# The first feed-forward group summed ahead of the norm, in the mixer projection's stage

## The reference, cut to what matters

```python
mixed = gates[:, :, 0] * y_ssm + gates[:, :, 1] * y_rwkv + gates[:, :, 2] * y_hgrn
x = x + mixed @ w_out[l]
h_gate, h_up = jnp.split(rmsnorm(x, norm2_w[l]) @ ffn_w_in[l], 2, axis=-1)
x = x + (jax.nn.silu(h_gate) * h_up) @ ffn_w_down[l]

def rmsnorm(x, w, eps=NORM_EPS):
    xf = x.astype(jnp.float32)
    y = xf * lax.rsqrt(jnp.mean(xf * xf, axis=-1, keepdims=True) + eps)
    return (y * w.astype(jnp.float32)).astype(x.dtype)
```

## Time and profile before

| | |
|---|---|
| median of 3 runs | 2075.53 us (2075.15 to 2080.94) |
| the profiled execution | 2076.96 us, span 2075.0 us |
| mean granted TensorE clock | 0.971 of full speed |
| TensorE busy | 1925.8 us, 93% of the span |
| VectorE, ScalarE busy | 1019.0 us (49%), 602.2 us (29%) |
| HBM traffic | 88 GB/s over the span |

### The profile page before, as it was taken

How to read it: one execution, slowest core, us unless ns; L and a number is a source line. 1 busy time by engine, 2 the same in 40 slices (tenths; PEclk the granted TensorE clock), 3 DMA queues, 4 the chain that set the end, 5 groups by cost and what they waited for, 6 DMA issues and landing times. The chain is left out here.

```text
span 2075.0 us, 40175 instructions
## 1 busy us (share of the span) xinstructions
PE 1925.8 (93%) x16700; PEld 1418.4 (68%) x16700; DVE 1019.0 (49%) x2050; ACT 602.2 (29%) x1287; POOL 75.3 (4%) x51
## 2 busy tenths in 40 slices
PE   6989999999999999998988799978898999989998
PEld 2566666666666666544666687767774998878887
DVE  3456666667676767312135568675445452311101
ACT  2234343434444443302023233233333220000000
POOL 0001010101010101000000000010000000000000
PEclk9999999999999999999999899989999999999999
DMA  9021213111111012022211433230002222534343
GB/s 379 24 83 45 100 52 104 41 63 41 33 42 32 32 42 73 1 92 101 102 66 41 156 122 122 83 121 33 33 33 112 82 82 81 183 122 149 139 178 142
DMA packets 52240, 184.73 MB, mean 89 GB/s; under 512 B 5856, under 2 KB 9312, under 8 KB 51552
## 3 DMA queue, kind: packets, MB, share of 16 engines
q1 hardware_dynamic: 52064, 182.23, 24.0%
HBM read 180.11 MB, written 2.10 MB: 88 GB/s over the span
## 5 line engine op out<-in xcount | busy, mean ns | idle before, releaser
L845 PE MATMUL banks<-u,w_ring 128*128 128x512 f32 x768 | 361.8, 603 | 2.0 <-DVE u L681 2.0
L386 PE MATMUL banks<-u,w_ring 128*128 128x256 f32 x1056 | 250.1, 389 | 8.4 <-PEq L195 8.4
L386 PEld LDWEIGHTS banks<-u,w_ring 128*128 128x128 f32 x1056 | 199.1, 195 | 41.9 <-issue 17.0
L845 PEld LDWEIGHTS banks<-u,w_ring 128*128 128x128 f32 x768 | 139.2, 192 | 124.5 <-issue 117.2
L410 PE MATMUL banks<-u,w_ring 128*128 128x256 f32 x704 | 155.0, 384 | 4.8 <-PEq L195 4.8
L410 PEld LDWEIGHTS banks<-u,w_ring 128*128 128x128 f32 x704 | 135.7, 193 | 24.0 <-issue 5.0
L3351 PE MATMUL banks<-gated,w_ring 128*128 128x512 f32 (+1 forms) x288 | 96.8, 498 | 1.8 <-PEq L195 1.8
L873 DVE SCALAR_TENSOR_TENSOR acc<-raw,hc,acc 128x512 f32<-128x512 f32 x128 | 96.2, 752 | 4.5
L3351 PEld LDWEIGHTS banks<-gated,w_ring 128*128 128x128 f32 x288 | 54.6, 190 | 44.1 <-issue 40.8
L3351 PE MATMUL banks<-ffn,w_ring 128*128 128x256 f32 x352 | 77.9, 385 | 3.0 <-PEq L195 3.0
L3201 DVE SCALAR_TENSOR_TENSOR ffn_tanh<-ffn_tanh,banks 128x256 f32<-128x256 f32 x22 | 9.2, 417 | 138.0 <-ACT ffn_tanh L3193 138.0
(11 more groups left out here) (500 smaller groups left out, 3202.0 us busy)
## 6 DMA issues: line engine op xcount, KB each, us to landing
w_ring<-in_w SPq DMA_DIRECT2D x289, 512.0 KB, 5.6
gated<-in_ada SPq DMA_DIRECT2D x32, 512.0 KB, 4.5
h<-in_h SPq DMA_DIRECT2D x2, 2048.0 KB, 9.6
const_base<-in_const SPq DMA_DIRECT2D x1, 1216.0 KB, 5.4
hold<-h SPq DMA_DIRECT2D x1, 1024.0 KB, 5.2
const_part<-in_const SPq DMA_DIRECT2D x1, 1024.0 KB, 4.9
h<-hold SPq DMA_DIRECT2D x1, 1024.0 KB, 9.6
out<-u SPq DMA_DIRECT2D x8, 128.0 KB, 1.9
```

The lines of the kernel that those rows point to most:

```text
L386: mm = self.nc.tensor.matmul(place, self.st.chunk(g % 2, slot)[:, P * k:P * k + P], self.src(k), start=(k == 0), stop=(k == KT - 1))
L845: mm = nc.tensor.matmul(self.places[m % len(self.places)][:, :], (st.slot(m) if g is None else st.chunk(g % 2, m))[:, P * k:P * k + P], u[ ...
```

## The change

A new tile `root` (128 x 256) is set aside. In `mixer_out` ScalarE also makes h x norm2_w for each of the 8 feature tiles and puts it into columns 0 to 255 of u. TensorE multiplies the first feed-forward group's four chunks with it, into banks 0 to 3: one tile, then the column sums; one tile, then the transposes; then two tiles more. ScalarE copies the spread root from bank 7 to `root`, and the eight products for u read it from there. `swiglu` has ten groups left. Its VectorE first multiplies the four finished banks with `root` and, with ScalarE's tanh, forms the first two tiles of the output. Banks are numbered anew so that the four are free when needed, and the ring's groups are split 7 and 10 where they were 6 and 11.

```diff
+        root = sb("root", [P, SEQ])
...
-def swiglu(nc, st, bank, src, out, th):
+def swiglu(nc, st, bank, src, out, th, root):
-    count = FF // 2
+    count = FF // 2 - 1
...
         def tensor(pe):
             def visit(g, h, r):
-                if not isinstance(g, int) or g >= 2:
-                    pe.wait_ge(s["done"], g * 2 - 2)
+                if not isinstance(g, int) or g >= 1:
+                    pe.wait_ge(s["done"], g * 2)
                 for m in range(4):
                     st.wait(pe, h, r, m)
-                    mm = accumulate(nc, bank[4 * h + m][:, 0:SEQ], [st.chunk(h, m)[:, P * k:P * k + P] for k in range(KT)],
+                    mm = accumulate(nc, bank[4 - 4 * h + m][:, 0:SEQ], [st.chunk(h, m)[:, P * k:P * k + P] for k in range(KT)],
...
         def scalar(act):
+            for m in range(2):
+                act.wait_ge(s["rooted"], 2 * m + 2)
+                nc.scalar.activation(out[:, m, :], th[:, 0, m, :], ACT.Tanh, scale=0.5).then_inc(s["rough_tanh"], 1)
...
         def vector(dve):
+            for m in range(2):
+                for up in range(2):
+                    nc.vector.tensor_tensor(th[:, up, m, :], bank[2 * up + m][:, 0:SEQ], root, ALU.mult).then_inc(s["rooted"], 1)
+            for m in range(2):
+                dve.wait_ge(s["rooted"], 2 * m + 2)
+                dve.wait_ge(s["rough_tanh"], m + 1)
+                nc.vector.scalar_tensor_tensor(out[:, m, :], out[:, m, :], 1.0, th[:, 0, m, :], ALU.add, ALU.mult).then_inc(s["doubled"], 1)
+                dve.wait_ge(s["doubled"], m + 1)
+                nc.vector.scalar_tensor_tensor(out[:, m, :], out[:, m, :], 0.5, th[:, 1, m, :], ALU.mult, ALU.mult).then_inc(s["done"], 1)
...
     units = [(b, m) for b in range(4) for m in range(KT)]
-    through = [0, 4, 8, 16, 24, 28, 32]
+    place = lambda q: (q + 4) % banks
+    through = [0, 4, 8, 16, 24, 28, 32, 33]
...
-        st.in_stage(6, 4, s["used"], block, through, {3: reload})
+        st.in_stage(7, 4, s["used"], block, through, {3: reload})
...
-            tail.sums(pe)
+
+            def rough(c):
+
+                st.wait(pe, 6 % 2, 6 // 2, c)
+                pe.wait_ge(s["evacuated"], len(units) - banks + c + 1)
+                for k in range(KT):
+                    if c == 0:
+                        pe.wait_ge(s["primed"], k + 1)
+                    mm = nc.tensor.matmul(bank[c][:, 0:SEQ], st.chunk(6 % 2, c)[:, P * k:P * k + P], u[:, k, 0:SEQ],
+                                          start=(k == 0), stop=(k == KT - 1))
+                return mm
+
+            rough(0)
+            pe.wait_ge(s["added"], KT - 1)
+            column_sums(nc, C, bank[7], tail.acc, tail.tiles).then_inc(s["sums"], 1)
+            rough(1)
+            pe.wait_ge(s["root"], 1)
+            spread(nc, C, bank[7], tail.rs, tail.tiles).then_inc(s["spread"], 1)
+            rough(2)
+            rough(3).then_inc(s["used"], 1)
 
         @block.scalar
         def _(act):
             link = Chain(act, s["act_own"])
             for k in range(KT):
+                act.wait_ge(s["evacuated"], 3 * KT + k + 1)
+                link(nc.scalar.activation(u[:, k, 0:SEQ], tail.tile(k), ACT.Copy, scale=g_cols[:, k:k + 1]), s["primed"])
                 tail.square(act, link, k)
+            act.wait_ge(s["spread"], 1)
+            link(nc.scalar.activation(root, bank[7][:, 0:SEQ], ACT.Copy), s["copied"])
...
             tail.mean(dve, link)
-            tail.scale(dve, link, u, g_cols)
-
-    st.passed(6, 4)
+            dve.wait_ge(s["copied"], 1)
+            tail.scale(dve, link, u, g_cols, root)
+
+    st.passed(7, 4)
```

More of the change, by code:

```diff
@@ L3143, in build @@
         with ExitStack() as es:
-            mixer_out(nc, st, bank, C, (ys, yr, yh), early, gates, h, hold, late, tail_work(SEQ, es), u, cc("norm2_w"))
+            mixer_out(nc, st, bank, C, (ys, yr, yh), early, gates, h, hold, late, tail_work(SEQ, es), u, cc("norm2_w"), root[:, :])
             nc.sync.sem_clear(late)
@@ L3150, in build @@
             ffn_tanh = sb("ffn_tanh", [P, 2, 2, SEQ], es)
-            swiglu(nc, st, bank, latent, ffn, ffn_tanh)
+            swiglu(nc, st, bank, latent, ffn, ffn_tanh, root[:, :])
             def add(m, ps, link, done):
@@ L3168, in build @@
         st.drain()
-def swiglu(nc, st, bank, src, out, th):
-    count = FF // 2
+def swiglu(nc, st, bank, src, out, th, root):
+    count = FF // 2 - 1
     st.begin(4)
-    with stage(nc, "used tanh doubled done") as (s, block):
+    with stage(nc, "rooted rough_tanh used tanh doubled done") as (s, block):
         def tensor(pe):
             def visit(g, h, r):
-                if not isinstance(g, int) or g >= 2:
-                    pe.wait_ge(s["done"], g * 2 - 2)
+                if not isinstance(g, int) or g >= 1:
+                    pe.wait_ge(s["done"], g * 2)
                 for m in range(4):
                     st.wait(pe, h, r, m)
-                    mm = accumulate(nc, bank[4 * h + m][:, 0:SEQ], [st.chunk(h, m)[:, P * k:P * k + P] for k in range(KT)],
+                    mm = accumulate(nc, bank[4 - 4 * h + m][:, 0:SEQ], [st.chunk(h, m)[:, P * k:P * k + P] for k in range(KT)],
                                     [src(k) for k in range(KT)])
@@ L3187, in scalar @@
         def scalar(act):
+            for m in range(2):
+                act.wait_ge(s["rooted"], 2 * m + 2)
+                nc.scalar.activation(out[:, m, :], th[:, 0, m, :], ACT.Tanh, scale=0.5).then_inc(s["rough_tanh"], 1)
             def visit(g, h, r):
                 act.wait_ge(s["used"], g + 1)
-                if not isinstance(g, int) or g >= 2:
-                    act.wait_ge(s["done"], g * 2 - 2)
+                act.wait_ge(s["done"], max(g * 2, 2) if isinstance(g, int) else g * 2)
                 for m in range(2):
-                    nc.scalar.activation(th[:, h, m, :], bank[4 * h + m][:, 0:SEQ], ACT.Tanh, scale=0.5).then_inc(s["tanh"], 1)
+                    nc.scalar.activation(th[:, 1 - h, m, :], bank[4 - 4 * h + m][:, 0:SEQ], ACT.Tanh, scale=0.5).then_inc(s["tanh"], 1)
             walk(act, count, visit)
         def vector(dve):
+            for m in range(2):
[7 more added lines that the diff above has]
+                nc.vector.scalar_tensor_tensor(out[:, m, :], out[:, m, :], 0.5, th[:, 1, m, :], ALU.mult, ALU.mult).then_inc(s["done"], 1)
             def visit(g, h, r):
@@ L3200, in visit @@
                     dve.wait_ge(s["tanh"], g * 2 + 2)
-                    nc.vector.scalar_tensor_tensor(th[:, h, m, :], th[:, h, m, :], 1.0, bank[4 * h + m][:, 0:SEQ],
+                    nc.vector.scalar_tensor_tensor(th[:, 1 - h, m, :], th[:, 1 - h, m, :], 1.0, bank[4 - 4 * h + m][:, 0:SEQ],
                                                    ALU.add, ALU.mult).then_inc(s["doubled"], 1)
-                    dve.wait_ge(s["doubled"], g * 2 + (m + 1))
-                    nc.vector.scalar_tensor_tensor(out[:, bass.ds(g * 2 + m, 1), :].rearrange("p a t -> p (a t)"), th[:, h, m, :], 0.5,
-                                                   bank[4 * h + 2 + m][:, 0:SEQ], ALU.mult, ALU.mult).then_inc(s["done"], 1)
+                    dve.wait_ge(s["doubled"], g * 2 + (m + 3))
+                    nc.vector.scalar_tensor_tensor(out[:, bass.ds(g * 2 + (2 + m), 1), :].rearrange("p a t -> p (a t)"), th[:, 1 - h, m, :],
+                                                   0.5, bank[6 - 4 * h + m][:, 0:SEQ], ALU.mult, ALU.mult).then_inc(s["done"], 1)
             walk(dve, count, visit)
-            dve.wait_ge(s["done"], 2 * count)
+            dve.wait_ge(s["done"], 2 * count + 2)
         st.groups(count, 4, s, block, ((block.tensor, tensor), (block.scalar, scalar), (block.vector, vector)))
@@ L3395, in residual_norm, with mixer_out @@
     st.passed(groups, per_body)
-def mixer_out(nc, st, bank, C, branches, early, gates, h, hold, reloaded, work, u, g_cols):
+def mixer_out(nc, st, bank, C, branches, early, gates, h, hold, reloaded, work, u, g_cols, root):
     banks = 6
     units = [(b, m) for b in range(4) for m in range(KT)]
-    through = [0, 4, 8, 16, 24, 28, 32]
+    place = lambda q: (q + 4) % banks
+    through = [0, 4, 8, 16, 24, 28, 32, 33]
     st.begin(4)
-    with stage(nc, "used mixed " + NormTail.NAMES) as (s, block):
+    with stage(nc, "used mixed primed copied " + NormTail.NAMES) as (s, block):
         tail = NormTail(nc, C, s, bank[7], h, CTX, SEQ, work, 3 * KT)
@@ L3431, in _ @@
                     at = k_tiles * (m % per_chunk) + k
-                    mm = nc.tensor.matmul(bank[q % banks][:, 0:SEQ], st.chunk(g % 2, c)[:, P * at:P * at + P],
+                    mm = nc.tensor.matmul(bank[place(q)][:, 0:SEQ], st.chunk(g % 2, c)[:, P * at:P * at + P],
                                           branches[b][:, k, :] if b < 3 else gates[:, k, :], start=(k == 0), stop=(k == k_tiles - 1))
                 mm.then_inc(s["used"], 1)
-            tail.sums(pe)
+            def rough(c):
[15 more added lines that the diff above has]
```

(3 more changed lines are left out.)

## The result

The changed kernel takes 2066.06 us as the median of 18 runs (2061.7 to 2071.71), the kernel before 2076.3 us (2073.46 to 2080.94, 18 runs beside them). The ratio is 0.9949 with a 95% interval of 0.9941 to 0.9957, so 10.6 us less, between 8.9 and 12.3. The two medians lie 10.2 us apart. The forecast was 2065.3 us, 10.2 us less.

A forecast was written before the change was run, and what follows sets the result against it. TensorE, busy 93%, bounds the kernel, with an 8.45 us pause before the feed-forward. Pause and 2.9 of clock go, 1.2 comes in: 10.2 us less, 2075.53 - 10.2 = 2065.3 us, own range 2064.2 to 2066.8.

The forecast's parts named there:

- Rough group and norm on TensorE: First feed-forward group, moved ahead of the norm: 13.81 us, plus 0.6 us for column sums and transposes among its matmuls.
- The three slacks: Time to spare beside the moved group: column sums 1.5 us, root before the transposes 2.2, end of VectorE's scaling 1.9.
- right-hand side 7: Last h x norm2_w product, by ScalarE: ready at 1820.7 us, first read by a matmul at 1822.6, cover 1.9 us.
- Boundary: From the last work of mixer_out to the start of the feed-forward stage: 0.6 us, bounds 0.5 and 1.4.
- Clock behind the boundary: TensorE's granted clock stays at 1.00 (2.4 GHz) from the feed-forward stage's first matmul, so 2.9 us of slow start goes.
- Ten groups: The feed-forward groups left in swiglu: 10 x 13.81 = 138.1 us, plus 0.2 for the last matmul's end and reaction.
- Down projection: Stage after the feed-forward: keeps its 3 us opening pause and the clock's fall, which cost 1.7 us.
- Rival 2: The clock doesn't fall at the down projection: 1.7 us more is won, 2063.6 us; chance 0.10.
- 3: The wait only moves: late sums, root or scaling hold TensorE; 2067 to 2070 us, or 2070 to 2072; chance 0.05.
- 4: Nothing happens, since the norm's chain was not what held TensorE: 2075.5 us; chance 0.01.
- 5: Slower: weight loads go out only when their group is due, TensorE waits 5.6 us for each; 2121 us; chance 0.03.
- rival 1: The clock falls at the new feed-forward boundary too, or the boundary is long: 2066.1 to 2069.0 us; chance 0.09.

The follow-up runs named there:

- The longer chain: Changed kernel with ScalarE's product h x column for the last feature tile made four times over; 2071.28 us in one execution, interval 153.8 us.
- changed kernel's second profile: The changed kernel, unaltered, run again beside the kernel with idle matmuls in two pauses; 2065.82 us, ratio 0.9941 to the kernel before.

## Why the prediction was right

By its own steps:

- **What bounds the kernel.** TensorE's pause was the place. Hiding it brought 7.4 of its 8.45 us, and the clock the rest. With the norm ahead of the group half of the gain in the interval was lost again (5.3 of 10.3 us), with the norm behind it three quarters (7.8 us).
- **Rough group and norm on TensorE**, forecast 13.81 + 0.6 us: 14.37 from tile 31 to the end of the last rough matmul. The column sums took 0.37 us of the stream (3.82 us from tile 0 to tile 1, instead of 3.45) and the transposes 0.30, not 0.22.
- **The three slacks**, forecast 1.5, 2.2 and 1.9 us: 1.2 (last addition done at 1822.66, column sums at 1823.84), 2.4 (root done at 1825.38, transposes at 1827.74) and 2.2. The first was over-estimated by 0.3 us: the forecast let the rough group begin with tile 31's addition, but its first matmul starts 0.27 us before it (1820.39 against 1820.66), and the column sums come that much earlier. The longer chain confirmed the smaller slack by sticking out 0.5 us at the sums. For right-hand side 7 the working writes 1820.06 + 0.51 = 1820.7, which is 1820.57; the missing 0.09 us is the gap between VectorE's addition and ScalarE's start, and with it the forecast of 1.0 us behind the start of the addition was met (1821.69 against 1820.66).
- **Boundary**, forecast 0.6 with bounds of 0.5 and 1.4: 0.45, just under the lower bound. Nothing has to be evacuated behind the last matmul.
- **Clock behind the boundary**, forecast 1.00: 1.00, in all five profiles with this boundary. The 2.9 us that I had put down to the clock were measured alone at 2.9. That they fit so closely is in part luck: a fall cost 1.7 us behind a pause of nearly the same length in another version, and the forecast had one profile to go by.
- **Ten groups**, forecast 138.1 + 0.2: 138.4 (1835.48 to 1973.89). The added vector work ended 3.0 us into the stage, long before anything waited for it.
- **Sum**: 153.3 forecast, 153.2 measured. The boundary came 0.15 us shorter and the ten groups 0.1 us longer than forecast.
- **Weights**: the next group's load went out at 1820.65, behind tile 31, and no matmul waited for w_ring.
- **Down projection**: its pause and its fall stayed, 91.8 us behind the last tanh in both. Rival 2 did not come about in the two profiles of the changed kernel. It did in that of the version with the transposes one tile later, which has the same feed-forward and down-projection stages: 90.1 us behind the last tanh (2065.4 - 1975.24). So it is a matter of the execution, as the rival had it.
- Rivals 1, 3, 4 and 5 did not come about either. The point behind rival 1 was closer than I thought: behind the boundary of 0.45 us the clock never fell, but behind the one of 1.89 us it did, in its one execution.

One number of the list of signs was off: the last tanh at 1973.89 and not 1973.0. The interval was as forecast; its start had moved.

## What to carry to other kernels

A norm whose factor is one number for each token can be multiplied in behind a matrix product, so matmuls with the un-normed values can cover the chain of the norm. Place its small matmuls between them where their inputs are just ready, and check the slack of each link from the timeline. A pause of TensorE is to be priced at its length plus the slow stretch that may follow; here that was 8.45 and 2.9 us, and 1.7 us for the slow stretch in other places. Where a pause couldn't be filled with work, the profiles with idle matmuls in it had no slow stretch behind it, and the idle matmuls cost nothing in the interval; only for the longest pause do the times confirm the gain.

## What the runs showed of the hardware

**Short pauses and the clock.** Pauses of 0.45, 0.99 and 1.40 us left the granted clock at 1.00 in the stretches looked at; one of 1.89 us, with full work on either side, was followed by 3.4 us at the 1.2 GHz level, which began 1.3 us after the work had resumed. I had not expected a fall from under 3 us. The start of the mixer projection shows it too: TensorE stands still three times there, for 0.98, 1.16 and 1.65 us with small matmuls between them (changed kernel's second profile, 1731.97 to 1737.05), and the clock fell in each of the nine profiles without idle matmuls. With the down projection's pause of 2.97 us the clock fell in seven profiles and not in the eighth. So no single length divides the two here. The Trainium skill (TensorE: Matmul & The Clock Gate, "A second HAM failure mode: psum-queue depth-cycling") tells of a kernel in which short idles between groups of matmuls came often enough to swing the clock. The start of the mixer projection, with its three idles in a row, agrees; the changed kernel's boundary of 0.45 us is a single one, and the clock stayed at 1.00.

**Identical code ahead of the change moves by 8 us.** Up to tile 31 the changed kernel, its second profile and five of the six experiments on it run the same instructions; the one with idle matmuls in two pauses is left out here. The addition for tile 31 started at 1820.66, 1821.93, 1826.93, 1821.97, 1824.74, 1818.88 and 1823.86 us. The windows show falls that one execution has and another has not. Before:

```profile
811.00:819.00 8.00, 7.24 (x153) 5.19 (x153) 3.39 (x5) 1.20 (x2) 0.00 (x0) 0.79 0.05 16
1490.00:1500.00 10.00, 7.47 (x201) 5.63 (x194) 6.97 (x16) 4.00 (x11) 0.00 (x0) 1.00 0.01 2
```

and the changed kernel, in the same stretches:

```profile
811.00:819.00 8.00, 7.42 (x219) 5.37 (x220) 4.35 (x7) 1.19 (x2) 0.00 (x0) 1.00 0.04 13
1490.00:1500.00 10.00, 7.93 (x166) 6.37 (x167) 6.67 (x15) 3.45 (x10) 0.00 (x0) 0.83 0.01 2
```

That falls differ between executions of one code fits the Trainium skill (TensorE: Matmul & The Clock Gate, "Part 1: The HAM clock gate"), which calls the monitor's window free-running. Such falls are not all of the spread: before tile 31 the changed kernel's first profile has 112.6 us at the 1.2 GHz level and its second 105.8 us, and yet tile 31 came later in the second (1821.93 against 1820.66). What makes up the rest is open. It means that a difference of 1 to 3 us is not to be read from spans here, and is to be read from an interval around the change.
